# An order of the work planned in the source, V rows shared out by it, and twelve diagonals instead of four, in a two-layer trunk with expert retrieval

## The reference, cut to what matters

```python
def _peer(h, w_q, sub_keys, u_tab, v_tab):
    ...
    def chunk(xc):                                   # 128 tokens
        q = (xc @ w_q).reshape(C, PEER_HEADS, 2, PEER_HALF)
        s = jnp.einsum('thpd,hpkd->thpk', q, sub_keys).astype(jnp.float32)
        sv, si = lax.top_k(s, PEER_TOPK)
        ...
        top, pos = lax.top_k(cand, PEER_TOPK)
        eidx = jnp.take_along_axis(cidx, pos, axis=-1)
        g = jax.nn.softmax(top, axis=-1)
        a = jnp.einsum('thkd,td->thk', u_tab[eidx], xc).astype(jnp.float32)
        w = (g * jax.nn.gelu(a)).astype(xc.dtype)
        return jnp.einsum('thk,thkd->td', w, v_tab[eidx])

def reference(x, ...):
    for l in range(DEPTH):
        h = _rms(x, g_mix_norm[l])
        x = x + _mixer_block(h, ...)
        h = _rms(x, g_ffn_norm[l])
        x = x + _peer(h, w_peer_q[l], peer_sub_keys[l], peer_u[l], peer_v[l])
    return x
```

## Time and profile before

| what | value |
|---|---|
| median of the runs | 3346.97 us (3340.78 to 3350.18, 3 runs) |
| the profiled execution, its own time | 3380.76 us |
| its span in the trace | 3379.0 us |
| mean TensorE clock granted in it | 0.873 |
| bytes moved by DMA | 1210.29 MB, 358 GB/s over the span |
| gathers | 2048 of 512 KB |

### The profile page before, as it was taken

How to read it: one execution, slowest core, us unless ns; L and a number is a source line. 1 busy time by engine, 2 the same in 40 slices (tenths; PEclk the granted TensorE clock), 3 DMA queues, 4 the chain that set the end, 5 groups by cost and what they waited for, 6 DMA issues and landing times. The chain is left out here.

```text
span 3379.0 us, 27583 instructions
## 1 busy us (share of the span) xinstructions
PE 2539.8 (75%) x7696; PEld 1429.3 (42%) x7696; DVE 2316.0 (69%) x5442; ACT 691.7 (20%) x1655; POOL 2305.9 (68%) x2052
## 2 busy tenths in 40 slices
PE   6559777986677877986877787986787877665666
PEld 5446344653354444643444444653354444222222
DVE  2495768667779985565768888556657978655554
ACT  2112311213311211122311222123322211101011
POOL 0256756666667777777777777676777777777776
PEclk9779889997788988997888889998898989788888
DMA  6489999998899999999999999999999999999998
GB/s 254 174 313 396 365 380 376 351 376 286 311 370 375 371 343 373 411 398 361 349 411 383 382 382 366 382 388 338 333 347 396 389 366 376 342 373 366 372 369 333
DMA packets 317239, 1210.29 MB, mean 358 GB/s; under 512 B 37280, under 2 KB 37536, under 8 KB 301728
## 3 DMA queue, kind: packets, MB, share of 16 engines
q0 software_dynamic: 294912, 1073.87, 84.0%
q1 hardware_dynamic: 22176, 134.66, 10.1%
HBM read 1206.29 MB, written 2.10 MB: 358 GB/s over the span
## 5 line engine op out<-in xcount | busy, mean ns | idle before, releaser
L830 PE MATMUL psY<-ring,diag 128*128 128x512 f32 x3120 | 1668.6, 679 | 635.6 <-ACT diag L669 287.9
L481 POOL DMA_INDIRECT ring<-in_u,idx x1024 | 1161.6, 1134 | 565.2 <-issue 296.9
L481 POOL DMA_INDIRECT ring<-in_v,idx x1024 | 1144.1, 1117 | 496.0 <-issue 282.5
L1092 DVE CUSTOM_DVE_ANT_0 ring<-ring,htok 128x1024 f32<-128x1024 f32 x1024 | 1228.5, 1223 | 259.9 <-DMA ring<-in_u,idx 200.8
L830 PEld LDWEIGHTS psY<-ring,diag 128*128 128x128 f32 x3120 | 637.6, 215 | 1449.3 <-issue 1218.4
L669 ACT ACTIVATE diag<-cst,wgt 128x128 f32<-128x128 f32 x780 | 275.9, 394 | 492.6 <-PE psY L830 170.0
L1101 DVE SCALAR_TENSOR_TENSOR x<-ring,wgt,x 128x1024 f32<-128x1024 f32 x244 | 313.9, 1286 | 28.7 <-DMA ring<-in_v,idx 25.3
L706 PE MATMUL psP<-wr,hT 128*128 128x256 f32 x1344 | 312.1, 387 | 16.2 <-issue 7.4
L702 PE MATMUL psP<-hT,wr 128*128 128x256 f32 (+1 forms) x1664 | 320.9, 351 | 0.7 <-ACT hT L519 0.7
L702 PEld LDWEIGHTS psP<-hT,wr 128*128 128x128 f32 x1664 | 283.5, 200 | 64.3 <-issue 38.7
L706 PEld LDWEIGHTS psP<-wr,hT 128*128 128x128 f32 x1344 | 261.5, 195 | 88.2 <-issue 43.5
(11 more groups left out here) (125 smaller groups left out, 1680.9 us busy)
## 6 DMA issues: line engine op xcount, KB each, us to landing
wr<-in_w_in SPq DMA_DIRECT2D x44, 1024.0 KB
wr<-in_w_q SPq DMA_DIRECT2D x40, 1024.0 KB
ring<-in_u,idx POOLq DMA_INDIRECT x1024
ring<-in_v,idx POOLq DMA_INDIRECT x1024
wr<-in_w_out SPq DMA_DIRECT2D x16, 1024.0 KB
ring<-in_w_in SPq DMA_DIRECT2D x11, 1024.0 KB, 16.6
probs<-in_subkeys SPq DMA_DIRECT2D x5, 1024.0 KB
ring<-in_w_out SPq DMA_DIRECT2D x4, 1024.0 KB, 17.8
```

Source lines behind the costliest of these rows:

```text
L481: pool.indirect_dma_start(out=ring[:, q % NB], out_offset=None, in_=table, in_offset=bass.IndirectOffsetOnAxis(ap=idx[:, s % NS, n:n + 1], ...
L830: last = nc.tensor.matmul(psY[:, b * 512:(b + 1) * 512], diag[:, m % ND], r[:, b * 512:(b + 1) * 512], start=first, stop=final)
L1092: v.tensor_tensor_reduce(out=r, in0=r, in1=htok[:, s % NS], scale=1.0, scalar=0.0, op0=ALU.mult, op1=ALU.add, accum_out=adot[:, J % 2, k:k ...
```

## The change

The slot tables go. At import, the source now runs `plan_orders`, a small event-driven planner with a cost in microseconds for each part (`cost`), the needs of each part (`needs`), the buffers that parts hold and free, and a model of the gathers and the loads. Each time an engine is free it picks, among all that can begin then, the one with the earliest due time: for front parts the old nominal times, scaled by `GROUPS` and `SLOT_US`; for rows the time of landing plus 5 us. The lists that come out (`ORDERS`) are what each engine's program runs through, in this fixed order. Which engine adds a V row also comes out of the planner (`ROW_BY`): VectorE now has 156 of the 1024 rows and TensorE 868. `ND` goes from 4 to 12 (eight more diagonals take as much memory as one place of `ring`), and `NB` from 20 to 19. `norm1` on VectorE no longer waits for the parameters; the parts that use them do. Two waits for `cat_squared` are added on VectorE, since parts of neighbouring steps can now stand closer. The instructions themselves are the same otherwise.

```diff
-NB = 20
+NB = 19
-ND = 4
+ND = 12
-GROUPS = [((0,), -72, 1.0, 1.0), ((1,), 22, 1.0, 0.95), ((2, 3), 126, 0.7, 1.2), ((4, 5), 336, 1.15, 1.3),
-          ((6, 7), 594, 0.97, 1.5)]
+GROUPS = [((0,), -72, 1.0, 1.0), ((1,), 2, 0.95, 0.95), ((2, 3), 126, 0.9, 1.15), ((4, 5), 340, 1.2, 1.25),
+          ((6, 7), 600, 1.1, 1.5)]
+SLOT_US = 2.65
+U_SLACK = 5.0
+V_SLACK = 5.0
+X_SLACK = 5.0
+PE_AHEAD = 3
+MARGIN = 1.0
+def plan_orders():
...
+    def queue_gathers():
+        while state["gather"] < len(plan):
+            q = state["gather"]
+            kind, J, k = plan[q]
+            if kind == "u" and k == 0 and ("dve", "top index", J // PH, J % PH) not in done:
+                return
...
+            if q >= NB and plan[q - NB] not in done:
+                return
+            t = max(state["pool"], now + 0.3)
+            state["pool"] = t + 1.25
+            state["dma"] = max(state["dma"], t + 2.6) + 1.25
+            at(state["dma"] + 0.3, "land", plan[q])
+            state["gather"] += 1
+    def choices(eng):
...
+            if missing[key] or ready[key] > now + 1e-9:
+                continue
...
+            c.append((due[key], key))
+        if eng == "dve":
...
+                    c.append((landed["u", J, k] + U_SLACK, ("u", J, k)))
...
+                if eng == "dve" and ("v", J, k) in landed:
+                    c.append((landed["v", J, k] + X_SLACK, ("v", J, k)))
+                if eng == "act" and diags["made"] - diags["used"] < PE_AHEAD and ("v", J, k) in landed:
+                    c.append((done["w", J], ("d", J, k)))
...
+        for eng in orders:
+            if busy[eng] is None:
+                c = choices(eng)
+                if c:
+                    begin(eng, min(c)[1])
-def vector_rows(J):
-    return BUSY_ROWS.get(J, (3, 7, 11, 15))
-        _by = int(_k in vector_rows(_J))
+        _by = ROW_BY[_J, _k]
@@ act
-            for J in range(HEADS + 1):
-                for k in range(TOPK):
-                    by, m = V_NO.get((J - 1, k), (1, 0))
-                    if by == 0:
-                        act.wait_ge(w_ready, J)
...
-                    for part, s, i in at_slot("act", J * TOPK + k):
-                        front(s, part, i)
+            for name, *where in ORDERS["act"]:
+                if name == "d":
+                    J, k = where
+                    m = V_NO[J, k][1]
+                    act.wait_ge(w_ready, J + 1)
+                    if m >= ND:
+                        act.wait_ge(v_used, m - ND + 1)
...
+                else:
+                    part, s, i = where
+                    front(s, part, i)
@@ dve
+                if c == 0 and part in ("qk", "conv", "sgu in", "sgu"):
+                    dve.wait_ge(s_par, N_PAR * (l + 1))
                 if part == "norm1":
-                    if c == 0:
-                        dve.wait_ge(s_par, N_PAR * (l + 1))
```

More of the change, by code:

```diff
@@ L75, in top_parts, with front_times @@
[L75 to L82, removed]
+SLOT_US = 2.65
[4 more added lines that the diff above has]
+MARGIN = 1.0
+def front_times(steps):
     p, a, n = [], steps[0], len(steps)
-    def add(parts, s):
-        p.extend((eng, t, part, s, i) for eng, t, part, i in parts)
@@ L106, in front_parts @@
         o = out + gap * i
-        add([("pe", o, "piece", N_IN + i), ("pe", o + n / 2, "rest of piece", N_IN + i), ("dve", o + 1.25 * n, "out", i)], a)
+        p += [(o, "pe", "piece", a, N_IN + i), (o + n / 2, "pe", "rest of piece", a, N_IN + i), (o + 1.5 * n, "dve", "out", a, i)]
     second = out + N_OUT * gap - 1
@@ L119, in front_parts @@
     return p, top
-def part_tables():
-    tables = {"act": [], "pe": [], "dve": []}
-    for steps, start, rate, top_rate in GROUPS:
[L126 to L133, removed]
@@ L136, in at_slot, with cost @@
-def at_slot(eng, slot):
-    return [row[1:] for row in PARTS[eng] if slot <= row[0] < slot + 1]
+def cost(eng, part, s, i):
+    n, w = len(GROUP_OF[s]), s % NC + 1
+    if part in ("piece", "rest of piece"):
+        if eng == "act":
+            return 0.3 * n
+        whole = CB <= i < N_IN or i >= N_IN + N_OUT
+        return 3.5 * n / 2 if whole or n == 2 else 3.5 if part == "piece" else 0.0
+    return {"pe": {"hT1": 1.1, "qk": 1.1, "catT": 1.1, "hT2": 1.1, "scores": 0.25 * w, "dil T": 0.15 * w, "dil out": 0.15 * w,
+                   "conv": 0.3, "sgu": 0.5, "logits": 1.2, "sums": 0.9 if i == 0 else 1.75, "stick out": 0.5 * w,
+                   "key scores": 0.5},
+            "act": {"norm1": 1.2, "norm2": 1.2, "hT1": 2.4, "catT": 2.4, "hT2": 1.1, "qk squares": 1.1, "qk taken": 1.3,
+                    "v squares": 0.4, "dil exp": 0.3 + 0.1 * w, "dil taken": 0.2 + 0.1 * w, "logits": 3.6, "stick exp": 0.7,
+                    "conv taken": 0.4, "cat squares": 1.1, "queries": 0.6, "key scores": 0.4, "gate exp": 1.7},
+            "dve": {"norm1": 2.9, "qk": 6.6, "bias": 0.3 + 0.3 * w, "weigh": 0.2 + 0.15 * w, "dil out": 0.6, "softplus": 1.3,
+                    "exponent": 1.2, "stick out": 0.4, "sgu in": 3.2, "sgu": 0.7, "conv": 2.6, "cat": 4.6, "out": 0.35 * n,
+                    "norm2": 4.4, "top keys": 3.0, "top pairs": 2.8, "top index": 2.9, "gate": 0.5}}[eng][part]
@@ L141, in numbers @@
+ORDERS, ROW_BY = plan_orders()
 def numbers(eng, *names):
-    rows = [row[1:] for row in PARTS[eng] if row[1] in names]
+    rows = [key[1:] for key in ORDERS[eng] if key[0] == eng and key[1] in names]
     return {row: n for n, row in enumerate(rows)}
@@ L1112, in _ @@
                     v.tensor_tensor(wgt[:, J % 2], gl[:], gate[:, s % NS, h * TOPK:(h + 1) * TOPK], ALU.mult).then_inc(w_ready, 1)
-                if J >= PH and J % PH == 0:
-                    add_peer(J // PH - 1)
+                elif where[0] == "x":
+                    add_peer(where[1])
+                else:
+                    part, s, i = where
+                    front(s, part, i)
 def kernel(x, g_mix_norm, w_in, w_sgu, b_sgu, g_sgu_v, g_q_dil, g_k_dil, conv_w, g_q_sb, g_k_sb, g_head_out,
```

478 lines of the change are left out of this document (385 added, 93 removed).

## The result

The changed kernel takes 3316.5 us in the median (3298.8 to 3324.6, 4 runs) where the kernel before, run beside it again, takes 3348.6 (3340.8 to 3362.6). The ratio is 0.990, with a 95% interval of 0.986 to 0.994: faster by 1.0%, or 32 us. 94 us were forecast, and a time between 3165 and 3350, with 3253 as the likeliest. The sign was right, the size was not, by a factor of three.

What follows compares the result with a forecast made beforehand. No engine was full; GpSimd's gathers were held by late consumers, VectorE's dots and TensorE's V rows, for 273 us. Terms -164 + 23 + 15 + 15 + 15 + 2 = -94 us, so 3347 - 94 = 3253 us, range 3165 to 3350.

Steps and rivals of the forecast that it cites:

- the first term: Order by readiness and twelve diagonals: takes 60% of GpSimd's 273 us of waits for ring places, -164 us.
- The rate rival: Heads 20 to 54 already at a transfer ceiling of 373 GB/s; only heads 1 to 15 gain: 3339 us, chance 0.05.
- The base: Whole kernel: -94 us against the profiled 3380.8; the median is 33.8 lower, so 3347 - 94 = 3253 us.
- Step 1's lump: Eight searches within U rows 97 to 112: VectorE needs 86 us, gathers 44, ring reserve 19; stall of +23 us.
- Head 16 without a lead: Head 16's first U row waits for `idx`, which comes only after head 15's last dot: +15 us.
- Group (2,3)'s searches: Sixteen searches on VectorE lie within 57 U rows, 80 before: excess of 26 or 5 us, taken as +15.
- 88 rows: V rows moved from VectorE to TensorE, 188 us more work there, mostly covered by idle time: +15 us, bounds 0 and 40.
- A burst of query pieces: At head 20, meeting no idle time of TensorE: named with the bounds 0 and 40 us of the V-row move.
- The rival in which TensorE binds throughout: Half of TensorE's 188 us more is on the path and the gain is gone: 3347 us, chance 0.08.
- The start: Before the first gathers: at most 3 us back from `norm1`, two query pieces cost 5.6 us: +2 us, bounds -3 and +6.
- The weights rival: In the lumps of searches, heads wait for query pieces, 8.1 us more each, 130 us: 3383 us, slower, chance 0.11.
- The rival in which the planner takes nearly all: Nearly all 273 us of ring waits go: 3155 us, between 3117 and 3171, chance 0.18.

Runs made afterwards that it cites:

- run with light consumers: Kernel before with dots, VectorE multiply-adds and V matmuls over 8 columns (first and last row of a step whole): 3083.6 us, one run, against 3222.6.
- The rows alone: Kernel before, slot order and 4 diagonals, with the planner's table of V rows (156 on VectorE instead of 244): 3237.1 against 3222.6 us, ratio 1.0047.

## Why the prediction was right or wrong, step by step

**The step that failed is the first term: the 273 us of ring waits read as time "in which GpSimd could have issued and was held by a consumer", and 60% of them taken as gain.** The mechanism holds: order by readiness makes the consumers early. The size does not. Outside the three places the change gave 128 us in the profiled pair, not 164. The split by place says where the term failed. For heads 1 to 15 the prediction named some 60 us of waits beside the stall, and 58 are left of 161. For the heads from 20 on it named 50 or less, and 75 are left beside the lump; with head 16 to 19 it is 89, where there were 112.

Two things were overlooked. First, most of those 112 us seem to belong to the chip. Here are the ring waits from head 16 to 62 on the second chip, with twelve diagonals in the kernel before, and they come to 26 us without 0.30 for each:

```profile
POOL ring L481 <- PE psY L830: 38.2, 71, 3.0
POOL ring L481 <- DVE adot L1092: 13.3, 13, 1.7
```

Second, a ring wait is not yet lost time. In the run with light consumers 325 us of such waits stand beside transfers at 408 GB/s in heads 22 to 54, with nothing lost. The text priced waits of GpSimd and never asked whether the DMA engines ran dry in them. Why so much of the waits after head 16 stays on the first chip is open in part: 40 of the 89 us are `remote`. It is not that the consumers wait for landings: during the ring waits of both traces that name a consumer, TensorE and VectorE are nearly always at work on rows or front parts, and wait for a landing for less than 3 us in all.

**The rate rival**, given 0.05, said 3339; 3316.5 was measured, and the forecast was 3253. Its pattern came: heads 1 to 15 gained 41 us (857.3 to 816.3), heads 20 to 54 gained 15 (1719.9 to 1705.1). Its ceiling of 373 GB/s did not: it is a mean, and the first and the fourth chip both have stretches of 5 us at 404 GB/s and more (lines of the first are in the last section). These are also above the 358 GB/s that the prediction cites from the Trainium skill, "DMA: Bandwidth & Descriptors", section "Where 436 GB/s comes from". On the second chip with light consumers the mean is 408 GB/s and heads 22 to 54 take 1492 us, where the twelve-diagonal kernel took 1544 and the change, on the third, 1510. On those chips the transfers leave little to win in these heads.

**The base.** The profiled execution of before was 33.8 us above its median; the forecast was a difference against it. The two traces differ by 57.8 us and the medians by 32; these 26 us are the difference of the two profiled runs from their medians (32.2 and 6.5 above). A trace 1% above the median may hold more ring waits than the typical run; how many of the 273 were of this kind is not shown.

**The terms for the searches.** Step 1's lump: +23 forecast, +22.8 measured, and the match is luck. The stall itself is three waits of 38.6 us; the stretch grew by less because its old ring waits, 22 us, were there before. The forecast stall came out small because it spread the eight searches over 16 U rows: with the 12 that the kernel has, the same sum gives 66 + 15 - 33 - 19 = 29. Head 16 without a lead: +15 forecast and +15.4 measured, with a wait of 20.3 us. Group (2,3)'s searches: +15 forecast, +0.9 measured, with five waits for dots of 12.2 us together. The two that fitted in size are not gains that can be had one by one: each fixed alone brought nothing that shows.

**TensorE.** +15 forecast for 88 rows, from their sum. The rows alone cost 15 us in the old order. What was missed is the lump at head 20 (+31.5), where two sets of transposes with waits for ScalarE and then input pieces of the next group stand ahead of one V row. A burst of query pieces there was named in a bound and priced as absorbed. The rival in which TensorE binds throughout did not come: it is busy 78% of the span, where the prediction looked for over 80.

**The start**: +2 forecast, -0.2 measured; first gather at 138.2 in both. **The weights rival** did not come: in heads 6 and 7 the long waits are for dots, while VectorE searches. **The rival in which the planner takes nearly all**, 3155 us, did not come either. TensorE's waits for diagonals fell from 287.9 to 145.3 us, as the prediction looked for.

In sum: -164 + 70 forecast, -128 + 70 in the traces, and -32 in the medians. The two 70s are alike by chance: the forecast one is 23 + 15 + 15 + 15 + 2, the measured one 22.8 + 15.4 + 31.5.

## What to carry to other kernels

A wait of the issuing engine for its consumers need not cost anything while the transfers have work: read the rate of the transfers over the same stretch before pricing the wait, and make the consumers light once to see what the pace is without them. Lumps in a planned order can be read from the order and priced against the ring's reserve (work in the lump, less the pace, less the reserve), but count the rows inside the lump exactly, and expect little from removing one stall of several that hang on the same due times. Price a change against a typical run, and if it can be had against a second chip, not against a single trace.

## What the runs showed of the hardware

The same program took 3223 to 3378 us on four chips. The rate that transfers reach at their best is the same: heads 55 to 62 run at 409 GB/s on average on the third chip (41.1 us per head in the change), and at 369 on the first (45.7), but there too stretches of 404 to 416 GB/s stand between slower ones. What the first and fourth chips show, and the second and third do not, is stops of TensorE. One of them in the profile of before, in windows of 5 us (busy us of TensorE, its weight loads, VectorE, ScalarE and GpSimd with instructions, then granted clock, DMA share, GB/s):

```profile
1570.00:1575.00 5.00, 4.90 (x17) 2.35 (x15) 3.12 (x7) 3.14 (x6) 3.78 (x5) 1.00 1.02 404
1585.00:1590.00 5.00, 0.58 (x2) 0.00 (x0) 0.00 (x0) 0.00 (x0) 3.78 (x5) 1.00 1.03 410
1590.00:1595.00 5.00, 0.00 (x0) 0.00 (x0) 0.00 (x0) 0.00 (x0) 3.78 (x5) 0.59 1.03 410
1595.00:1600.00 5.00, 0.00 (x0) 0.00 (x0) 0.00 (x0) 0.00 (x0) 0.88 (x1) 0.50 1.02 408
1600.00:1605.00 5.00, 3.46 (x7) 2.10 (x8) 4.16 (x6) 2.07 (x6) 3.43 (x3) 0.50 0.56 161
```

TensorE's records end at 1585.6, and the results that ScalarE and VectorE wait for, recorded at 1582.7 to 1583.7, reach them at 1600.8. Both have then stood idle for 18 us and more; the gathers go on at 410 GB/s until the ring is full, and only then does the rate fall. Waits marked `remote`, as those for such a late signal are, stand in all six traces of the first and fourth chips and in none of the eight of the other two. Stretches over 2 us in which TensorE, VectorE and ScalarE all idle sum to 78 us in the profile of before and 69 in that of the change (after the first gather), and to 12 and 7 us in one trace each of the second and third chips. What stops TensorE is not shown, nor whether this is all of the difference between the chips.

GpSimd's gather instruction is lengthened by what VectorE does: 1.13 us on average, 1.00 with dots over 8 columns, 1.10 with V rows over 8 columns, 0.95 with all consumers light (one trace each, the last on the second chip). The Trainium skill, "SBUF — State Buffer", section "Who interferes with whom", says that a VectorE instruction with two inputs in SBUF contends with a GpSimd instruction that reads SBUF; the runs agree in direction. How much it is depends on more than the dots' number: in heads 55 to 62 of the change on the third chip, with whole dots, the mean is 0.98. And a shorter instruction alone brought no time: with light dots heads 22 to 54 took the same 1624 us.
